# Context tokens' up-projection: four PSUM banks, weights rounded ahead of the conv, gates one product later

## The reference

```python
def dwconv3(u, w, b):
    up = jnp.pad(u, ((0, 0), (1, 1), (0, 0)))
    return up[:, :-2] * w[0] + up[:, 1:-1] * w[1] + up[:, 2:] * w[2] + b

def conv_ffn(h, w_up, w_c, b_c, w_down):
    u = dwconv3(h @ w_up, w_c, b_c)
    gate, val = jnp.split(u, 2, axis=-1)
    return (jax.nn.silu(gate) * val) @ w_down
...
        if not last:
            fc = rmsnorm_2(ctx, g_pre_ffn[i]) * (1.0 + csc2) + csh2
            yc = conv_ffn(fc, w_up[i], w_ffn_conv[i], b_ffn_conv[i], w_down[i])
            ctx = ctx + cga2 * rmsnorm_2(yc, g_post_ffn[i])
```

## Time and profile before

| | |
|---|---|
| median of 3 runs | 2721.55 us (2718.03 to 2723.92) |
| profiled execution | 2711.67 us, its span 2709.8 us |
| TensorE busy | 2424.4 us, 89% of the span |
| VectorE busy | 1670.2 us, 62% |
| ScalarE busy | 1033.9 us, 38% |
| GpSimd busy | 712.8 us, 26% |
| HBM | 95 GB/s over the span |

### The profile page before, as it was taken

One profiled execution on the slowest core, in us unless ns is written; L12 is line 12 of the kernel. 1 busy time (PEld: TensorE's weight loads), 2 busy tenths in 40 slices (PEclk: granted clock), 3 DMA queues, 4 the chain that ended last, 5 costly groups with the idle time before them and its releaser, 6 DMA issues.

```text
span 2709.8 us, 37944 instructions
## 1 busy us (share of the span) xinstructions
PE 2424.4 (89%) x11870; PEld 1859.5 (69%) x11870; DVE 1670.2 (62%) x3180; ACT 1033.9 (38%) x1728; POOL 712.8 (26%) x542
## 2 busy tenths in 40 slices
PE   5999876999877888997998889999979989899996
PEld 3767544866646767887675668888857567688885
DVE  6868668868769667754547546563153583656512
ACT  3333453233453435544324334443233251444421
POOL 2201134211124334354110142223421003222233
PEclk9989988999988899998999999999999999999998
DMA  4523213432224323454221013323232101132321
GB/s 153 194 86 109 71 49 128 169 117 104 71 78 143 101 71 125 154 159 151 86 86 48 1 63 93 101 93 101 94 115 84 70 1 47 63 100 93 101 94 62
DMA packets 71529, 259.44 MB, mean 96 GB/s; under 512 B 7873, under 2 KB 9314, under 8 KB 69444
## 3 DMA queue, kind: packets, MB, share of 16 engines
q1 hardware_dynamic: 71364, 257.42, 28.4%
HBM read 255.29 MB, written 2.10 MB: 95 GB/s over the span
## 4 chain that ended last, share of the span: by engine, by line
PE 69%; DVE 13%; issue 9%; ACT 6%; POOL 1%; DMA 1%; DVEq 0%; ACTq 0%; SPq 0%; POOLq 0%
PE banks L969 6%; PE banks L971 6%; PE banks L965 6%; PE banks L994 4%; PE banks L988 4%; PE banks L987 4%; PE banks L703 3%; PE banks L704 3%; PE banks L708 3%; PE banks L480 2%; PE banks L863 2%; PE banks L481 2%; PE banks L485 2%; PE banks L882 2%; PE banks L893 2%
## 5 line engine op out<-in xcount | busy, mean ns | idle before, releaser
L1983 POOL TENSOR_TENSOR wl_t<-ring,wh_t 128x512 fp32r<-128x512 f32 x132 | 222.0, 1684 | 508.6 <-ACT wh_t L1240 508.6
L1441 DVE CUSTOM_DVE_ANT_0 banks<-m_t 128x512 f32<-128x512 f32 x384 | 314.2, 818 | 11.4 <-issue 0.7
L2025 POOL TENSOR_TENSOR wl_t<-ring,wh_t 128x512 fp32r<-128x512 f32 x132 | 170.9, 1295 | 488.2 <-ACT wh_t L1350 488.1
L1664 DVE TENSOR_TENSOR wl_t<-ring,wh_t 128x512 fp32r<-128x512 f32 x132 | 102.8, 781 | 226.6 <-ACT wh_t L1240 222.6
L1926 POOL TENSOR_TENSOR wl_t<-ring,wh_t 128x512 fp32r<-128x512 f32 x72 | 110.8, 1541 | 442.3 <-ACT wh_t L1058 442.2
L480 PE MATMUL banks<-xh_t,wh_t 128*128 128x512 f32 x512 | 209.1, 408 | 7.3 <-DVE y_t L1612 5.2
L969 PE MATMUL banks<-xh_t,wl_t 128*128 128x512 f32 (+1 forms) x960 | 204.2, 355 | 6.8 <-DVE wl_t L1868 6.8
L965 PE MATMUL banks<-xh_t,wh_t 128*128 128x512 f32 (+1 forms) x960 | 204.7, 355 | 5.7 <-DVEq L1865 5.6
L481 PE MATMUL banks<-xl_t,wh_t 128*128 128x512 f32 x512 | 202.9, 396 | 0.0
L971 PE MATMUL banks<-xl_t,wh_t 128*128 128x512 f32 (+1 forms) x960 | 202.9, 354 | 0.0
L1240 ACT ACTIVATE wh_t<-ring 128x1024 fp32r<-128x1024 f32 x132 | 138.9, 1054 | 162.7 <-PE banks L994 162.4
(11 more groups left out here) (344 smaller groups left out, 4940.6 us busy)
## 6 DMA issues: line engine op xcount, KB each, us to landing
ring<-w_d SPq DMA_DIRECT2D x338, 512.0 KB, 3.5
m_t<-wmod_d SPq DMA_DIRECT2D x96, 512.0 KB, 3.5
qh_t<-tables_d SPq DMA_DIRECT2D x6, 1024.0 KB, 4.7
m_t<-tables_d SPq DMA_DIRECT2D x6, 1024.0 KB, 6.9
par<-p_d SPq DMA_DIRECT2D x4, 696.0 KB, 4.7
x_t<-x_in_d SPq DMA_DIRECT2D x1, 2048.0 KB, 11.4
big<-tables_d SPq DMA_DIRECT2D x2, 1024.0 KB
out_d<-x_t SPq DMA_DIRECT2D x1, 2048.0 KB, 7.1
```

What stands on the lines that cost most here:

```text
L1441: nc.vector.tensor_tensor_reduce(out=mod_scratch, in0=MRING[i % RM][:, half * 512:(half + 1) * 512], in1=cbc[:, w * D + half * 512:w * D + ...
L1983: pool.tensor_tensor(WL[j % 2][:, 0:512], slot2(j)[:, 0:512], WH[j % 2][:, 0:512].bitcast(F32), ALU.subtract).then_inc(sm2["w2_lo_a"], 1)
L2025: pool.tensor_tensor(WL[q % 2][:, 0:512], slot2(24 + q)[:, 0:512], WH[q % 2][:, 0:512].bitcast(F32), ALU.subtract).then_inc(sm2["w2_lo_a"], 1)
```

## The change

For the context tokens only, the up-projection's products go over the four banks 0, 1, 4 and 5 in turn instead of two; TensorE waits for a bank's release of the product four before, and for the third and fourth product not at all. ScalarE does the rounding of the next weights first and the conv's middle tap behind it. VectorE does its half of the low weights first and the side taps behind it. The gate's sigmoid and the two multiplications come behind the next gate's product, its rounding and low part behind the next value's. ScalarE's and VectorE's context loops are written out over the 44 products. For the 512 tokens the same instructions stay, now in the `else` branches (left out below with the removed loops, which are the same lines further left). The opening pair `product_pair(28, 22)` stays as it is.

```diff
@@ -695,9 +695,10 @@
                 def sum_begin(which):
                     pe.wait_ge(*at2("sum2_read", which))
-                def product3(i, j):
-                    dst, hi, lo, xh, xl = acc(i), WH[j % 2], WL[j % 2], v["XH"], v["XL"]
+                def product3(i, j, bank=None):
+                    dst = acc(i) if bank is None else bank
+                    hi, lo, xh, xl = WH[j % 2], WL[j % 2], v["XH"], v["XL"]
                     pe.wait_ge(*at2("w2_hi", j + 1))
                     for k in range(KD):
                         pe.matmul(dst, hi[:, k * P:(k + 1) * P], xh[k], start=k == 0, stop=False)
@@ -950,17 +951,19 @@
                     mm = pe.matmul(ps[2][:, 0:n], ones, v["H"][c], start=c == 0, stop=c == KD - 1)
                 mm.then_inc(sm2["x2_summed"], 1)
                 product_pair(28, 22, lambda k: at2("xh2", 8 + k + 1), lambda k: at2("xl2", 8 + k + 1))
+                banks = (0, 1, 4, 5) if is_ctx else (0, 1, 0, 1)
+                back = 1 if is_ctx else 0
                 for q in range(2, 4):
-                    product3(28 + q, 22 + q)
+                    product3(28 + q, 22 + q, ps[banks[q]][:, 0:n] if is_ctx else None)
                 with pe.Fori(1, FK // 2) as g:
                     for q in range(4):
                         def later(name, i, step):
                             sem, val = at2(name, i)
                             pe.wait_ge(sem, g * step + val)
                         i, hi, lo, xh, xl = 28 + q, WH[q % 2], WL[q % 2], v["XH"], v["XL"]
-                        later(f"acc2_{i % 2}_free", i // 2, 2)
+                        later(f"acc2_{i % 2}_free", i // 2 - back, 2)
                         later("w2_hi", 22 + q + 1, 4)
-                        dst = ps[i % 2][:, 0:n]
+                        dst = ps[banks[q]][:, 0:n]
                         for k in range(KD):
                             pe.matmul(dst, hi[:, k * P:(k + 1) * P], xh[k], start=k == 0, stop=False)
                         later("w2_lo_a", 22 + q + 1, 4)
@@ -1332,31 +1335,58 @@
...
+                def gate_sigmoid(p):
+                    act.wait_ge(*at2("conv2", 6 + 2 * p + 2))
+                    nc.scalar.activation(v["SG"][p % 2], v["AG"][p % 2], ACT.Sigmoid).then_inc(sm2["gate_sig2"], 1)
+                def gate_high(p):
+                    act.wait_ge(*at2("gt2", p + 1))
+                    nc.scalar.activation(v["GH"][p], v["SG"][p % 2], ACT.Copy).then_inc(sm2["gh2"], 1)
+                if is_ctx:
+                    for t in range(2 * FK):
+                        w_high(24 + t)
+                        p = t // 2
+                        dst, c = (v["AG"] if t % 2 == 0 else v["AV"])[p % 2], p + FK * (t % 2)
+                        act.wait_ge(*at2("acc2", 28 + t + 1))
+                        act.wait_ge(*at2("g_ready", p - 2 + FSTART))
+                        nc.scalar.activation(dst, ps[(0, 1, 4, 5)[t % 4]][:, 0:n], ACT.Identity, bias=p2c(P_FCB + c),
+                                             scale=p2c(P_FCW + 2 * FK + c)).then_inc(sm2["conv_mid"], 1)
+                        if t % 2 == 0 and p >= 1:
+                            gate_sigmoid(p - 1)
+                        if t % 2 == 1 and p >= 1:
+                            gate_high(p - 1)
+                    gate_sigmoid(FK - 1)
+                    gate_high(FK - 1)
...
@@ -1847,35 +1877,73 @@
...
+                def conv_ctx(t):
+                    p = t // 2
+                    dst, c, bank = (v["AG"] if t % 2 == 0 else v["AV"])[p % 2], p + FK * (t % 2), ps[(0, 1, 4, 5)[t % 4]]
+                    dve.wait_ge(*at2("conv_mid", 6 + t + 1))
+                    nc.vector.scalar_tensor_tensor(dst[:, 1:n], bank[:, 0:n - 1], p2c(P_FCW + c), dst[:, 1:n],
+                                                   ALU.mult, ALU.add).then_inc(conv_left[0], 1)
+                    dve.wait_ge(conv_left[0], t + 1)
+                    nc.vector.scalar_tensor_tensor(dst[:, 0:n - 1], bank[:, 1:n], p2c(P_FCW + 4 * FK + c), dst[:, 0:n - 1],
+                                                   ALU.mult, ALU.add).then_inc(sm2["conv2"], 1)
+                    dve.wait_ge(*at2("conv2", 6 + t + 1))
+                    dve.sem_inc(sm2[f"acc2_{t % 2}_free"], 1)
+                def gate_products(p):
+                    sg = v["SG"][p % 2]
+                    dve.wait_ge(*at2("gate_sig2", p + 1))
+                    nc.vector.tensor_tensor(sg, sg, v["AG"][p % 2], ALU.mult).then_inc(sm2["gate_mul2"], 1)
+                    dve.wait_ge(*at2("gate_mul2", p + 1))
+                    nc.vector.tensor_tensor(sg, sg, v["AV"][p % 2], ALU.mult).then_inc(sm2["gt2"], 1)
+                def gate_low(p):
+                    dve.wait_ge(*at2("gh2", p + 1))
+                    nc.vector.tensor_tensor(v["GL"][p], v["SG"][p % 2], v["GH"][p].bitcast(F32), ALU.subtract).then_inc(sm2["g_ready"], 1)
+                if is_ctx:
+                    for t in range(2 * FK):
+                        w_low(24 + t)
+                        conv_ctx(t)
+                        if t % 2 == 0 and t >= 2:
+                            gate_products(t // 2 - 1)
+                        if t % 2 == 1 and t >= 3:
+                            gate_low(t // 2 - 1)
+                    gate_products(FK - 1)
+                    gate_low(FK - 1)
...
```

More of the change, by code:

```diff
@@ new lines, in gate_high @@
+                def gate_high(p):
[16 more added lines that the diff above has]
+                    gate_high(FK - 1)
+                else:
+                    with act.Fori(0, FK // 2) as g:
+                        for q in range(4):
+                            i = 28 + q
+                            dst = (v["AG"] if q % 2 == 0 else v["AV"])[q // 2]
+                            c = g * 2 + q // 2 + FK * (q % 2)
+                            sem, val = at2("acc2", i + 1)
@@ new lines, in run2, with later @@
+                if is_ctx:
[8 more added lines that the diff above has]
+                    gate_low(FK - 1)
+                else:
+                    with dve.Fori(0, FK // 2) as g:
+                        def later(name, i, step):
+                            sem, val = at2(name, i)
+                            dve.wait_ge(sem, g * step + val)
+                        for q in range(4):
+                            i = 28 + q
+                            dst = (v["AG"] if q % 2 == 0 else v["AV"])[q // 2]
+                            c = g * 2 + q // 2 + FK * (q % 2)
+                            later("conv_mid", 6 + q + 1, 4)
+                            nc.vector.scalar_tensor_tensor(dst[:, 1:n], ps[i % 2][:, 0:n - 1], par2[:, bass.ds(P_FCW + c, 1)], dst[:, 1:n],
+                                                           ALU.mult, ALU.add).then_inc(conv_left[0 if is_ctx else 1], 1)
+                            dve.wait_ge(conv_left[0 if is_ctx else 1], g * 4 + (q + 1 if is_ctx else l * 2 * FK + q + 1))
+                            nc.vector.scalar_tensor_tensor(dst[:, 0:n - 1], ps[i % 2][:, 1:n], par2[:, bass.ds(P_FCW + 4 * FK + c, 1)], dst[:, 0:n - 1],
+                                                           ALU.mult, ALU.add).then_inc(sm2["conv2"], 1)
+                            later("conv2", 6 + q + 1, 4)
+                            dve.sem_inc(sm2[f"acc2_{i % 2}_free"], 1)
+                            later("w2_hi", 24 + q + 1, 4)
+                            nc.vector.tensor_tensor(WL[q % 2][:, 512:1024], slot2(24 + q)[:, 512:1024], WH[q % 2][:, 512:1024].bitcast(F32),
+                                                    ALU.subtract).then_inc(sm2["w2_lo_b"], 1)
+                            if q % 2:
+                                p, sg = q // 2, v["SG"][q // 2]
+                                later("gate_sig2", p + 1, 2)
+                                nc.vector.tensor_tensor(sg, sg, v["AG"][p], ALU.mult).then_inc(sm2["gate_mul2"], 1)
+                                later("gate_mul2", p + 1, 2)
+                                nc.vector.tensor_tensor(sg, sg, v["AV"][p], ALU.mult).then_inc(sm2["gt2"], 1)
+                                later("gh2", p + 1, 2)
+                                nc.vector.tensor_tensor(gl_t[:, bass.ds((g * 2 + p) * n, n)], sg, gh_t[:, bass.ds((g * 2 + p) * n, n)].bitcast(F32),
+                                                        ALU.subtract).then_inc(sm2["g_ready"], 1)
```

60 lines of the change are left out of this document (13 added, 47 removed).

## The result

Five runs of the changed kernel have a median of 2691.16 us (2685.99 to 2699.30), five of the kernel before, taken with them, 2718.03 (2714.83 to 2723.92). The ratio is 0.9897 with a 95% interval of 0.9871 to 0.9923: 28 us less, between 21 and 35. The forecast was 23.1 us less. It was made from a base of 2721.55, the median of three runs; on the base of five the ratio stands for 2690.0 us, a microsecond under the low end of the range, 2691.

What follows compares the result with a forecast made beforehand. PE, busy 89%, loses time in the context up-projection to stalls on bank release and low weights; 22.15 us of stalls + 0.8 entry + 0.15 exit = 23.1 us, from the 2721.55 us median to 2698.4 us; range 2691 to 2709.

## What to carry to other kernels

Where three engines go round in a ring, the wait that the trace names is where the delay surfaces: before picking what to remove, write down each engine's list for one round with its times from one event, for the new order, and look at who starts first on the shared port and by how much. A change of several parts can be worth more than its parts, which each alone can be a loss; test by turning one back, not only by doing one alone. And where the whole time spreads by more than the effect, take a span between two events of the changed stage, and read the granted clock over it: in the two profiles of the changed kernel at the full clock it repeats to 0.01 us while the runs spread by 6 to 19, and a fall of the clock inside it moved six of the experiments by 0.8 us, as much as the smallest differences between them.

## What the runs showed of the hardware that I had not expected

The same instructions behind waits that are written out have shorter distances than in a loop whose waits go by the turn: on VectorE 1.15 us for two side taps to the next instruction instead of 1.33, and 0.48 instead of 0.71 us of waiting for ScalarE's rounding of the gate, 4.7 us over 42 products. That the loop's waits are the cause was not tested by itself.

An idle VectorE starts 0.04 us behind ScalarE's end and GpSimd 0.08 (1058.47 and 1058.51 behind 1058.43), so an idle VectorE won each time. 0.47 us of further work on an engine with 0.94 us of idle time in a pair cost 1.03 us a pair.

Unchanged code ahead of the stage ended anywhere between 1034 and 1051 us, and the one stretch compared, 242.88 against 245.44 us, had the granted clock at 1.00 and 0.92 in its first ten microseconds.

Behind the same 2.26 us of idle time of PE the same 48 matmuls of the opening pair ran at 1.00 throughout in seven of the thirteen profiles (6.35 to 6.37 us) and fell to 0.50 inside in the six others (7.17 to 7.19 us). Over whole executions of the changed kernel, 0.959 went with spans of 2684.3 and 2689.4 us and 0.953 with 2697.5.
